# Moving the small constants of an SBUF layout, so that every split tile lies 384 bytes modulo 512 from the weights

## The reference, cut to what matters

```python
# every norm, then a product with a weight matrix
u = rmsnorm(h, g); proj = u @ w_in
g, up = jnp.split(hn @ w_gate_up, 2, axis=-1)          # 1024 x 5632
h = h + rmsnorm((jax.nn.silu(g) * up) @ w_down, ...)   # 2816 x 1024
```

## Time and profile before

| | |
|---|---|
| median of 3 runs | 2263.9 us |
| the profiled execution: time / span | 2265.19 us / 2263.3 us |
| TensorE busy (matmul) | 2236.3 us, 99% of the span |
| VectorE / ScalarE / GpSimd busy | 55% / 41% / 10% |
| granted TensorE clock | 0.999 of full |
| chain that ended last | TensorE 87%, VectorE 8%, ScalarE 2%, issue 2%, GpSimd 1% |

### The profile page before, as it was taken

One profiled execution on the slowest core, in us unless ns is written; L12 is line 12 of the kernel. 1 busy time (PEld: TensorE's weight loads), 2 busy tenths in 40 slices (PEclk: granted clock), 3 DMA queues, 4 the chain that ended last, 5 costly groups with the idle time before them and its releaser, 6 DMA issues.

```text
span 2263.3 us, 29343 instructions
## 1 busy us (share of the span) xinstructions
PE 2236.3 (99%) x11388; PEld 1819.1 (80%) x11388; DVE 1254.1 (55%) x1842; ACT 938.1 (41%) x1507; POOL 235.0 (10%) x218
## 2 busy tenths in 40 slices
PE   9999999999999999999999999999999999999999
PEld 7887888898888888876778888888886668888887
DVE  6467656345444226998664444333989654544433
ACT  5545454354333234226954333222333963433322
POOL 3000032020000001022030000001003122000001
PEclk9999999999999999999999999999999999999999
DMA  5221033123222322221122222222321112322232
GB/s 215 105 75 57 20 131 131 38 75 112 93 93 93 112 94 95 85 93 44 51 75 94 98 106 93 93 104 93 112 75 56 48 66 75 130 93 93 93 112 74
DMA packets 29909, 203.20 MB, mean 90 GB/s; under 512 B 3440, under 2 KB 4080, under 8 KB 6128
## 3 DMA queue, kind: packets, MB, share of 16 engines
q1 hardware_dynamic: 28512, 197.34, 24.5%
q10 hardware_dynamic: 1296, 4.46, 0.5%
HBM read 199.69 MB, written 2.10 MB: 89 GB/s over the span
## 4 chain that ended last, share of the span: by engine, by line
PE 87%; DVE 8%; ACT 2%; issue 2%; POOL 1%; DMA 0%; ACTq 0%; POOLq 0%; DVEq 0%
PE bank L415 25%; PE bank L417 25%; PE bank L416 25%; DVE cy L2352 3%; PE bank L999 1%; PE bank L2130 1%; PE bank L2117 1%; PE bank L2107 1%; DVE w_lo L301 1%; PE bank L970 1%; POOL acc L324 1%; PE bank L987 1%; PE bank L2007 1%; PE bank L1590 1%; PE bank L1567 1%
## 5 line engine op out<-in xcount | busy, mean ns | idle before, releaser
L415 PE MATMUL bank<-x_hi,w_hi 128*128 128x512 f32 (+1 forms) x2032 | 790.0, 389 | 6.3 <-DVE w_lo L301 2.7
L417 PE MATMUL bank<-x_hi,w_lo 128*128 128x512 f32 (+1 forms) x2032 | 775.1, 381 | 0.0
L416 PE MATMUL bank<-x_lo,w_hi 128*128 128x512 f32 (+1 forms) x2032 | 774.1, 381 | 0.0
L301 DVE TENSOR_TENSOR w_lo<-w_raw,w_hi 128x2048 fp32r<-128x2048 f32 x167 | 386.5, 2315 | 404.9 <-ACT w_hi L297 404.9
L297 ACT ACTIVATE w_hi<-w_raw 128x2048 fp32r<-128x2048 f32 x167 | 319.7, 1916 | 586.7 <-PE bank L417 584.9
L415 PEld LDWEIGHTS bank<-x_hi,w_hi 128*128 128x128 f32 x2032 | 382.2, 188 | 84.7 <-issue 6.8
L417 PEld LDWEIGHTS bank<-x_hi,w_lo 128*128 128x128 f32 x2032 | 382.0, 188 | 74.6
L416 PEld LDWEIGHTS bank<-x_lo,w_hi 128*128 128x128 f32 x2032 | 382.5, 188 | 72.5 <-issue 2.9
L415 PE MATMUL bank<-f_hi,w_hi 128*128 128x512 f32 (+1 forms) x572 | 215.2, 376 | 0.0
L416 PE MATMUL bank<-f_lo,w_hi 128*128 128x512 f32 (+1 forms) x572 | 215.0, 376 | 0.0
L417 PE MATMUL bank<-f_hi,w_lo 128*128 128x512 f32 (+1 forms) x572 | 215.0, 376 | 0.0
(11 more groups left out here) (354 smaller groups left out, 2650.9 us busy)
## 6 DMA issues: line engine op xcount, KB each, us to landing
w_raw<-w_d SPq DMA_DIRECT2D x184, 1024.0 KB, 4.8
out_d<-h SPq DMA_DIRECT2D x4, 512.0 KB, 6.1
h<-x_d ACTq DMA_DIRECT2D x3, 512.0 KB, 9.2
tab<-rope_d ACTq DMA_DIRECT2D x2, 640.0 KB, 3.9
memT<-mem_d ACTq DMA_DIRECT2D x1, 1024.0 KB, 4.9
w_raw<-w_d SPq DMA_DIRECT2D x2, 256.0 KB, 4.2
h<-x_d ACTq DMA_DIRECT2D x2, 256.0 KB, 6.0
w_raw<-w_d SPq DMA_DIRECT2D x1, 512.0 KB, 6.5
```

Of the source, the lines that this page charges most:

```text
L301: dve.tensor_tensor(w_lo[:, u.slot, :], w_raw[:, u.slot, :], w_hi[:, u.slot, :], ALU.subtract).then_inc(lo_ready, 1)
L415: pe.matmul(dst, wh[:, k, cols], hi[:, kx_, at:at + width], start=start, stop=False)
L416: pe.matmul(dst, wh[:, k, cols], lo[:, kx_, at:at + width], start=False, stop=False)
L417: return pe.matmul(dst, wl[:, k, cols], hi[:, kx_, at:at + width], start=False, stop=stop)
```

## The change

The constants that came after `sq` are placed first, ahead of `w_raw`, except `ident_b` (256 bytes) and `neg_sink` (128 bytes), which are placed between `w_lo` and `h`. The cursor ahead of `w_raw` is rounded up to a multiple of 128. Ahead of `cy` the cursor is moved up to the next place that is a multiple of 512 bytes from `scope`. The padding of three tiles' rows is halved. No instruction is added, removed or reordered; shapes and semaphores stay as they are.

```diff
+        gains = place("gains", [P, PACK_W])
+        ident = place("ident", [P, P])
+        ones = place("ones", [P, P])
+        mask_b = place("mask_b", [P, 2 * P], BF16)
+        eps_c = place("eps_c", [P, 3])
+        picks = place("picks", [P, QB * QB])
+        rcol, rcol_mem = place("rcol", [P, QB]), place("rcol_mem", [P, 2])
+        rcol_c, rcol_ln = place("rcol_c", [P, QB]), place("rcol_ln", [P, QB])
+        rcol_head = place("rcol_head", [P, 9 * QB * 2])
+        small = place("small", [P, 64])
+        jcol = place("jcol", [P, 64])
+        where[0] = (where[0] + 127) // 128 * 128
         w_raw = place("w_raw", [P, SLOTS, UNIT])
         w_hi = place("w_hi", [P, SLOTS, UNIT], F32R)
         w_lo = place("w_lo", [P, SLOTS, UNIT], F32R)
+        ident_b = place("ident_b", [P, P], BF16)
+        neg_sink = place("neg_sink", [P, LAYERS, 16])
         h = place("h", [P, DT, T])
...
         sq = place("sq", [P, 2, T])
-        gains = place("gains", [P, PACK_W])
-        ident = place("ident", [P, P])
...
-        jcol = place("jcol", [P, 64])
         scope = where[0]
...
         la = place("la", [P, 4, PAD + T], F32, a)
+        a[0] += (scope - a[0]) % (P * 4)
         cy_at = a[0]
...
-        lsq = place("lsq", [P, 2, T + 8], F32, b)
-        lcos = place("lcos", [P, 2, T + 8], F32, b)
+        lsq = place("lsq", [P, 2, T + 4], F32, b)
+        lcos = place("lcos", [P, 2, T + 4], F32, b)
...
-        lprob = place("lprob", [P, 4, 2, 2 * P + 4], F32, b)
+        lprob = place("lprob", [P, 4, 2, 2 * P + 2], F32, b)
```

## The result

The kernel after the change takes 2291.2 us (median of 4 runs, 2289.95 to 2291.7) against 2264.3 us for the kernel before on the same chip: ratio 1.0119, 95% interval [1.0105, 1.0133]. It is slower by 27 us, where 2251 us had been forecast. The first rival has happened: `x` lost its pace.

The account below looks back on a forecast made before the run. TensorE's matmuls, one after another, were taken as the bound. At 226.6 ns, `f` -9.6, `o` -3.0 and `c` -0.8 us, with 0.4 left unused, gave -13 us: 2251 us against the 2263.9 median, range 2244 to 2256.

Parts of the forecast that it names:

- The first rival: 512-wide `x` streams lose their good difference of 0 and slow down; 2299 us or 2278 us; chance 0.26.
- What bounds the kernel: Whole kernel: TensorE busy 2236.3 of 2263.3 us and hardly kept waiting, so the pace of its matmuls sets the time.
- The difference of the two reads as the cause: TensorE streams: pace depends on moving minus loaded address, modulo 512; `f` at 192 is 6.6 ns slower than `x` at 0.
- Which value between: 512-wide streams at the new difference 384: chose 226.6 ns, between bounds of 216 and about 235 ns.
- The lower bound of the pace: 512-column streams at 384: no faster than 216 ns, taken from float32 matmuls of L1567 and L1590.
- the second rival: 512-wide streams become faster: 220 ns and 2202 us, or 223.3 ns and 2227 us; chance 0.18.
- Half width: 256-wide matmuls: -5.2 us if all run at 113.6 ns, +2.6 us if all at 120; taken as 0.
- full step: `x` slows by 6.6 ns on 5616 matmuls to the pace of `f`: +35 us, 2299 us; chance 0.13.
- mixture: `x` streams mix paces and slow by 3.4 ns on 5616 matmuls: +14 us, 2278 us; chance 0.13.
- decision point of 229 ns: Pace of `x` from which its loss, 13 us, eats all that `f` and `o` gain.
- range of 8 in 10: Whole kernel: 2225 to 2281 us, leaving out the largest pace steps on both sides (0.21).
- The third: Rival: layout does nothing, `x` and `f` differ in pace for another reason; 2263.9 us; chance 0.09.

Follow-up runs that it names:

- all at 0: The change with `ident_b` and `neg_sink` also ahead of the weights, so every split tile lies 0 modulo 512 from them; 2253.8 us, ratio 0.9951 to the kernel before.
- all at 448: The change's layout with `gains` and `neg_sink` between `w_lo` and `h`, every split activation tile 448 modulo 512 behind the weights; 2293.6 us, ratio 1.0125 to the kernel before.

## Why the prediction was wrong

**What bounds the kernel** was right: the waits stayed as they were, and 25.0 of the 25.8 us are in the gaps of `x` alone.

**The difference of the two reads as the cause** was right. Moving everything leaves every pace (2264.2 us), changing the difference of `x` alone moves the full-width pace of `x` alone (of the rest, only the half-width `m` shifts, by 0.9 us one way and 0.9 the other), and splitting the weight tiles gives a cycle of three. That argues against the rule that I had weighed: the Trainium skill, "SBUF — State Buffer", section "SBUF: two separate sides", has TensorE never wait on anyone, and by it all these layouts would take one time. They run from 2252.8 to 2297.5 us. The rule speaks of waits on other engines, and between the matmuls of a stream the traces indeed show none. That TensorE's own two reads are in each other's way in the memory is my reading. What is shown is the dependence on the addresses, not the part of the chip in which it arises.

**"*Which value between*" is the step that failed.** It took 226.6 ns for 384, from two single matmuls, and from the claim that 384 "lies between 320 and 512 (= 0), both of which keep the short duration". Three things in it were wrong:

- A single matmul ahead of another load did not tell the pace of a stream at its difference. The 388 ns at 320 stood behind a stream at difference 0; I read them as that stream's state. With all tiles at 320 the stream has 228.9 ns, and the group of L417 393 ns:

```profile
L417 PE MATMUL bank<-x_hi,w_lo 128*128 128x512 f32 x1872 | 736.4, 393 | 0.0
```

- The period is 256 bytes, so 384 is 128, the far side from 0, and not a place between two good ones.
- A multiple of 64 isn't enough to hold one fixed pace: 64, 128, 384 and 448 all settle into cycles of several matmuls.

**The lower bound of the pace** was a misreading as well. The prediction took the 216 ns of L1567 for a row of 512 columns. In the trace its matmuls are 256 columns wide, two records for each call, and start 216 ns apart; plain float32 rows that are 512 wide, as those of L2025, start 429 ns apart. From the kernel before:

```profile
L2025 PE MATMUL bank<-lq,perm_q 128*128 128x512 f32 x32 | 15.6, 599 | 0.0
L1567 PE MATMUL bank<-kx,qx 128*128 128x256 f32 x64 | 15.1, 379 | 0.0
```

So no stream had shown that matmuls of 512 columns can start faster than 226.6 ns apart, and the second rival lost its ground with it. The sum of the forecast did not use this bound.

**The terms.** `x`: forecast 0, measured +25.0 us. `f`: -9.6 forecast, -1.4 measured; `o`: -3.0, -0.5; `c`: -0.8, +0.1. For `x`, `f` and `o` the cause is one, 232.4 ns in place of 226.6; the runs of `c` are too short to settle and keep 231.8 to 231.9 ns. Half width: forecast 0 between -5.2 and +2.6; `m`, `f` and `x`, moving and loaded, together gave +3.2, a little above the upper end, since the moving `m` has 293 ns of duration, more than any row of before at this width, and alone lost 1.7 us. The gaps of the float32 matmuls became 0.6 us shorter, within their +-1; L1567 keeps 1.73 us for 8, as in the earlier trace rows:

```profile
410.51 1.73 PE bank L1567 x8
```

**The rivals.** The first gave +35 us for the full step and +14 for the mixture. The truth, +27, is between, a little nearer the full step: its place and direction are right, and the stream is well beyond its decision point of 229 ns. The full step had a chance of 0.13 and lay outside the range of 8 in 10. Its full step was too large, since `x` gains 5.05 ns over its 5484 close gaps (27.7 us / 5484), not 6.6. The cycle of seven has 232.4 ns, not 233.2. And the steps just after an interruption were slow already: the first nine of each close run of `x` have 230.4 ns in the mean before and 232.3 after the change, the later ones 226.7 and 232.5. The second rival (220 ns) is seen at none of the nine differences run at full width. The third fell with all at 0: `f` came down to 226.67 ns in its own loop.

**The chances.** I gave 0.47 to the one value that the weakest evidence chose. Of the eight differences now run with all tiles alike, beside 384 itself, two (0, 256) are faster than before, two (64, 320) are 1 and 3 us above it, which is hardly clear of the noise, and four (32, 128, 448, 480) are slower by 29 to 34 us. In the earlier trace rows every full-width stream of another difference than 0 was slower, and I should have let that count for more than two single durations.

## What to carry to other kernels

Where TensorE is busy all the time and its groups of one shape have unequal durations (389 and 394 ns here), look at the addresses: for matmuls of 512 columns put the moving tile at a multiple of 256 bytes from the loaded one, here worth 0.5% against a layout with a part of the tiles so placed and 1.6% against one with none. Take the pace of a layout from a stream of at least some tens of matmuls at that very difference; here the single matmul behind a stream had the 388 ns that its own difference doesn't give in a stream. A 32-byte rounding of tile sizes is enough to lose the place, so align after every odd-sized constant, and keep both weight tiles at one difference.

## What the runs showed of the hardware

The paces are those of the long streams; at half width the activations move.

| difference, all tiles | pace, 512 wide | steps, ns | pace, 256 wide | us |
|---|---|---|---|---|
| 0 | 226.67 | even | 120.0 | 2253.8 |
| 256 | 226.67 | even | 120.0 | 2253.7 |
| 64 | 228.89, seldom 233.3 | 226, 229, 232 | 117.8 or 113.3 | 2265.5 |
| 320 | the same | the same | 117.8 or 113.3 | 2266.8 |
| 128 | 232.4 or 233.3 | cycle of 7, or 229, 238 | 118.7, `m` also 120.0 | 2292.7 |
| 384 (the change) | 232.4, seldom 233.3 | cycle of 7, or 229, 238 | 118.7, `f` 120.0 | 2291.2 |
| 448 | 233.33 | 231, 236, or even | 113.3, seldom 117.8 | 2293.6 |
| 32 | 233.33 | cycle of 4 or 12 | 116.7, `m` also 117.8 | 2297.5 |
| 480 | 233.33 | cycle of 2 | 118.3 | 2294.6 |

- The pace of an `fp32r` stream isn't a fixed sum of a matmul's cost; it is a pattern into which the stream settles. The total of each repeating cycle is a multiple of 6.67 ns: 1 x 34 units at 0, 3 in 103 at 64, 7 in 244 at 384, 2 in 70 at 448, 3 in 105 with `neg_sink` between the weight tiles.
- At 0 a stream takes up to ten matmuls after an interruption until its steps are even. It can settle in more than one pattern at the same difference: in the kernel with all at 448 some streams of `x` alternate between 231 and 236 ns and others have an even 233.3; `m` loaded at 320 had 117.8 ns before and 113.3 with only `x` moved.
- The two widths want different places: 0 and 256 are the best for 512 columns and the slowest for 256 (120.0), and 448 is the best for 256 columns (113.3) and among the slowest for 512.
- Plain float32 matmuls (L1567) keep 216 ns for a record of 256 columns in every layout. The Trainium skill, "TensorE: Matmul & The Clock Gate", section "Back-to-back issue gap", gives 215.8 ns for 512 columns, as the gap of an isolated matmul. No row here has it: `fp32r` streams of 512 columns never came below 226.67 ns, and plain float32 records of 512 columns take 429.
- Open: why the best `fp32r` pace is 34 units and not 33, and what fixes the choice among patterns. No run here tells that.
